# A two-layer encoder trunk: the pooling's scale and bias arrive as single rows and are spread by TensorE, the first filler matmuls run on a memset tile, and the constant table moves to SP's queue

## The reference, cut to what matters

```
h = rms_norm(x, norm_mix[0])
pooled[g] = mean of h over the last 2/4/8/16 tokens - h      # four groups of 256 channels
mixed[g]  = pooled[g] @ pool_w[g] + pool_b[g]                 # 256 x 256 per group
x = x + mixed * pool_scale                                    # pool_b and pool_scale: 1024 numbers each
h = rms_norm(x, norm_ffn[0]); x = x + (silu(h @ w1) * (h @ w3)) @ w2
```

## Time and profile before

| | |
|---|---|
| median of three runs | 1173.79 us |
| lowest, highest | 1169.85, 1173.88 us |
| the profiled execution: its own time | 1170.22 us |
| its span | 1168.4 us |
| TensorE matmul busy | 93% of the span |
| VectorE, ScalarE, GpSimd busy | 28%, 20%, 3% |
| HBM read | 414.09 MB, 356 GB/s over the span |

### The profile page before, as it was taken

How to read it: one execution, slowest core, us unless ns; L and a number is a source line. 1 busy time by engine, 2 the same in 40 slices (tenths; PEclk the granted TensorE clock), 3 DMA queues, 4 the chain that set the end, 5 groups by cost and what they waited for, 6 DMA issues and landing times.

```text
span 1168.4 us, 25208 instructions
## 1 busy us (share of the span) xinstructions
PE 1090.7 (93%) x11721; PEld 616.5 (53%) x11721; DVE 328.9 (28%) x455; ACT 236.6 (20%) x370; POOL 39.4 (3%) x35
## 2 busy tenths in 40 slices
PE   7999999999999999999999869999997889999776
PEld 6888888889763354364455215333632444364233
DVE  5655555458660040040032004002200310050023
ACT  5586555656620000000000000000000000000002
POOL 3000000011000000000000000000000000000000
PEclk9999999999999999999999999999999899999989
DMA  9986556534379999999999999999999999999994
GB/s 349 386 300 208 184 193 203 180 126 158 119 306 411 423 404 425 426 421 427 423 429 421 425 429 419 428 424 429 420 425 426 422 426 424 427 424 423 428 423 163
DMA packets 58562, 417.88 MB, mean 358 GB/s; under 512 B 5730, under 2 KB 11924, under 8 KB 34004
## 3 DMA queue, kind: packets, MB, share of 16 engines
q1 hardware_dynamic: 56656, 411.21, 86.3%
q0 software_dynamic: 1440, 4.46, 1.0%
q10 hardware_dynamic: 356, 0.54, 0.1%
HBM read 414.09 MB, written 2.10 MB: 356 GB/s over the span
## 4 chain that ended last, share of the span: by engine, by line
PE 64%; DMA 33%; SPq 2%; DVE 1%; issue 0%; ACT 0%; DVEq 0%
DMA weights<-in_moe_w 32%; PE psum L865 23%; PE psum L908 13%; PE psum L771 8%; PE psum L773 8%; PE psum L772 8%; SPq L682 1%; DMA raw<-in_pool_w 1%; PE psum L991 1%; PE psum L779 0%; PE psum L1112 0%; PE psum L883 0%; PE psum L1089 0%; SPq L673 0%; PE psum L1058 0%
## 5 line engine op out<-in xcount | busy, mean ns | idle before, releaser
L865 PE MATMUL psum<-weights,xg 128*32 128x512 f32 (+1 forms) x5072 | 494.8, 549 | 52.7 <-DMA weights<-in_moe_w 52.6
L865 PEld LDWEIGHTS psum<-weights,xg 128*32 128x32 f32 x5072 | 176.6, 111 | 368.4 <-issue 325.8
L908 PE MATMUL psum<-weights,hid_t 128*32 128x256 f32 x4480 | 247.7, 379 | 6.1 <-DMA weights<-in_moe_w 6.0
L908 PEld LDWEIGHTS psum<-weights,hid_t 128*32 128x32 f32 x4480 | 148.8, 110 | 99.8 <-DMA weights<-in_moe_w 9.1
L1718 DVE TENSOR_TENSOR sil<-sil,psum 128x1536 f32<-128x1536 f32 (+3 forms) x16 | 21.1, 1321 | 500.2 <-PE psum L865 499.5
L1572 DVE TENSOR_TENSOR low<-raw,high 128x2048 fp32r<-128x2048 f32 x50 | 114.3, 2286 | 95.5 <-ACT high L1276 95.3
L1276 ACT ACTIVATE high<-raw 128x2048 fp32r<-128x2048 f32 x51 | 97.8, 1917 | 54.4 <-PE psum L773 51.0
L1342 ACT ACTIVATE y_hi<-psum 128x768 fp32r<-128x768 f32 (+1 forms) x7 | 5.0, 719 | 488.6 <-PE psum L908 488.6
L771 PE MATMUL psum<-high,a_hi 128*128 128x512 f32 x224 | 87.3, 390 | 0.9 <-DVE a_lo L1609 0.9
L773 PE MATMUL psum<-low,a_hi 128*128 128x512 f32 x224 | 87.2, 389 | 0.0
L772 PE MATMUL psum<-high,a_lo 128*128 128x512 f32 x224 | 87.2, 389 | 0.0
(11 more groups left out here) (246 smaller groups left out, 676.1 us busy)
## 6 DMA issues: line engine op xcount, KB each, us to landing
weights<-in_moe_w SPq DMA_DIRECT2D x128, 1792.0 KB, 36.0
weights<-in_moe_w SPq DMA_DIRECT2D x47, 2048.0 KB, 38.7
raw<-in_ffn_w SPq DMA_DIRECT2D x42, 1024.0 KB, 8.7
weights<-in_moe_w SPq DMA_DIRECT2D x16, 1024.0 KB, 38.0
raw<-in_w_q SPq DMA_DIRECT2D x4, 1024.0 KB, 5.1
raw<-in_w_o SPq DMA_DIRECT2D x4, 1024.0 KB, 4.9
weights<-in_moe_w SPq DMA_DIRECT2D x4, 512.0 KB, 35.6
x_res<-in_x SPq DMA_DIRECT2D x2, 512.0 KB, 5.4
```

The source lines that it names most:

```text
L865: mm = pe.matmul(UP[c][g * BLK:(g + 1) * BLK, r, :], xg[:, k_, r * BLK:(r + 1) * BLK], w[:, g], start=k_ == 0, stop=k_ == DT - 1)
L908: mm = pe.matmul(Y[g * BLK:(g + 1) * BLK, to, :], hid_t[c][:, r, at_:at_ + BLK], w[:, b, g * GW:(g + 1) * GW], start=i == 0 and b == 0 and ...
```

## The change

- The table leaves ACT's queue and is issued on SP's, behind the band matrices.
- `pool_scale` and `pool_b` are no longer copied to 128 partitions. Each is loaded as one row of 4 KB into partition 0, by ACT's queue, as its first two DMAs.
- VectorE fills a new tile `filler` (128 x 256) with ones, ahead of its two small memsets, and multiplies the two rows on partition 0 before the norm.
- TensorE starts when the filler is written: two matmuls of 256 columns on it; a wait for the rows; two matmuls of 512 columns that spread the scale over 128 partitions (a row of ones against the row) into banks 6 and 7; a wait for VectorE's product; two that spread the product into banks 4 and 5; three more fillers. The eight matmuls on the identity are gone.
- ScalarE copies the spread product from banks 4 and 5 to `pool_bs`; its two copies of the scale to PSUM are gone, and so is GpSimd's product.
- The turned vectors go to bank 3 rather than 5, so TensorE waits for their copy before its seventh pair of pooling matmuls; it waits for ScalarE's copy of the product before the mixing matmuls.

```diff
+        filler = at("filler", [P, SEQ], F32, o_w + 8 * K)
...
             sp.dma_start(raw[slot(U_BAND)][:, 0:len(WINDOWS) * BAND], bands).then_inc(landed[slot(U_BAND)], 16)
+            sp.dma_start(consts[:, 0:C_COS], table[:, 0:C_COS]).then_inc(consts_in, 16)
             vector_loads(sp, 0, 2)
-            sp.dma_start(pool_rows[:, 1, :], bc(pool_scale[0])).then_inc(scale_in, 16)
             load(U_POOLW, pool_w.rearrange("o g (k p) f -> p (o g k) f", p=P), 8)
-            sp.dma_start(pool_rows[:, 0, :], bc(pool_b.rearrange("o g d -> (o g d)"))).then_inc(pool_in, 16)
...
-            pool.wait_ge(scale_in, 16)
-            pool.wait_ge(pool_in, 16)
-            pool.tensor_tensor(pool_bs[:], pool_rows[:, 0, :], pool_rows[:, 1, :], ALU.mult).then_inc(pool_ready, 1)
-            pool.wait_ge(pool_ready, 1)
+            pool.wait_ge(bias_copied, 1)
             pool.wait_ge(xn_ready, NT)
             pool.tensor_tensor(x_res[:, 1, :], x_res[:, 1, :], pool_bs[:], ALU.add).then_inc(pool_ready, 1)
...
+            def fill(n):
+                for _ in range(n):
+                    pe.matmul(banks[0][:, 0:SEQ], filler[:, 0:P], filler[:], start=True, stop=True)
+            pe.wait_ge(dve_step, 1)
+            fill(2)
+            pe.wait_ge(rows_in, 32)
+            for half in range(2):
+                pe.matmul(banks[OUT[1][half]][:], filler[0:1, 0:P], pool_rows[0:1, 1, half * CW:(half + 1) * CW],
+                          start=True, stop=True).then_inc(rows_spread, 1)
+            pe.wait_ge(dve_step, 3)
+            for half in range(2):
+                pe.matmul(banks[OUT[0][half]][:], filler[0:1, 0:P], pool_bs[0:1, half * CW:(half + 1) * CW],
+                          start=True, stop=True).then_inc(rows_spread, 1)
+            fill(3)
             pe.wait_ge(consts_in, 16)
-            keep_warm(0, 8)
             pe.wait_ge(xn_ready, NT)
...
+                if d == 5:
+                    pe.wait_ge(gains_ready, 1)
                 if d == 0:
                     pe.wait_ge(vec_in, 16 * 7)
-                    pe.transpose(banks[5][:, 0:NV], vec_rows[:, :], ident[0:NV, 0:NV]).then_inc(vec_turned, 1)
+                    pe.transpose(banks[3][:, 0:NV], vec_rows[:, :], ident[0:NV, 0:NV]).then_inc(vec_turned, 1)
             pe.wait_ge(pooled, DT // 2)
             pe.wait_ge(landed[slot(U_POOLW)], 16)
-            pe.wait_ge(gains_ready, 1)
+            pe.wait_ge(bias_copied, 1)
...
-            act.dma_start(consts[:, 0:C_COS], table[:, 0:C_COS]).then_inc(consts_in, 16)
-            act.wait_ge(dve_step, 1)
+            act.dma_start(pool_rows[0:1, 1, :], pool_scale[0].rearrange("(o n) -> o n", o=1)).then_inc(rows_in, 16)
+            act.dma_start(pool_rows[0:1, 0, :], pool_b.rearrange("o g d -> o (g d)")).then_inc(rows_in, 16)
+            act.wait_ge(dve_step, 2)
             warm(ACT.Sqrt)
             vector_loads(act, 2, 7)
             norm(0, lambda t: (x_in[t], 16))
-            act.wait_ge(scale_in, 16)
-            for half in range(2):
-                act.activation(banks[OUT[1][half]][:], pool_rows[:, 1, half * CW:(half + 1) * CW],
-                               ACT.Copy).then_inc(scale_spread, 1)
+            act.wait_ge(rows_spread, 4)
+            act.activation(pool_bs[:], psum[:, OUT[0][0] * CW:(OUT[0][1] + 1) * CW], ACT.Copy).then_inc(bias_copied, 1)
...
+            step(dve.memset(filler[:], 1.0))
             dve.memset(eps, EPS)
             step(dve.memset(warm_in, 1.0))
+            dve.wait_ge(rows_in, 32)
+            step(dve.tensor_tensor(pool_bs[0:1, :], pool_rows[0:1, 0, :], pool_rows[0:1, 1, :], ALU.mult))
...
-                dve.wait_ge(scale_spread, h + 1)
+                dve.wait_ge(rows_spread, h + 1)
...
-            dve.wait_ge(pool_ready, 1)
+            dve.wait_ge(bias_copied, 1)
             step(dve.tensor_tensor(x_res[:, 0, :], x_res[:, 0, :], pool_bs[:], ALU.add))
```

More of the change, by code:

```diff
@@ L408, in trunk_program @@
         x_in = [sem(f"x_in{t}") for t in range(NT)]
-        consts_in, vec_in, pool_in = sem("consts_in"), sem("vec_in"), sem("pool_in")
+        consts_in, vec_in, rows_in = sem("consts_in"), sem("vec_in"), sem("rows_in")
         misc_in, bo_in, rope_in = sem("misc_in"), sem("bo_in"), sem("rope_in")
@@ L421, in trunk_program @@
         pool_ready, pooled, mixed = sem("pool_ready"), sem("pooled"), sem("mixed")
-        scale_in, scale_spread, w_scaled = sem("scale_in"), sem("scale_spread"), sem("w_scaled")
+        rows_spread, w_scaled, bias_copied = sem("rows_spread"), sem("w_scaled"), sem("bias_copied")
         pooled_even, pooled_odd = sem("pooled_even"), sem("pooled_odd")
@@ L1743, in _ @@
             dve.wait_ge(vec_turned, 1)
-            dve.tensor_copy(gains[:], banks[5][:, 0:NV]).then_inc(gains_ready, 1)
+            dve.tensor_copy(gains[:], banks[3][:, 0:NV]).then_inc(gains_ready, 1)
             dve.wait_ge(gains_ready, 1)
@@ L1762, in _ @@
                 if t:
-                    dve.wait_ge(pool_ready, 2)
+                    dve.wait_ge(pool_ready, 1)
                 for half in range(2):
```

## The result

The changed kernel is slower: 1175.37 us median (1174.39 to 1176.48, 11 runs) against 1172.36 for the kernel before (1169.85 to 1173.88, 11 runs). The ratio is 1.003, with a 95% interval of 1.0021 to 1.0038, which is 2.5 to 4.5 us. The forecast was a gain of 0.85. The time lies inside the range that was given, and inside 0.5%, but on the other side: what came true is the first rival, by its clock that stays low.

What follows compares the result with a forecast made beforehand. The start chain to the first dense matmul was taken to bound, passing through one for one; weights gain 1.30, but TensorE's pooling limits mixing's gain to 0.85, so median 1173.79 - 0.85 = 1172.9 us, range 1168.5 to 1176.2.

Steps and rivals of the forecast that it cites:

- the first rival: Late rows (+2.3 us) or a clock that stays low (+2.7) make TensorE's start the bound; both +5.2; chance 0.22.
- The bound, and one for one to the end: TensorE's progress releases the late weight stream, so what the first 25 us win or lose reaches the end in full.
- the rise of the clock: TensorE's start: fast level after some 3.5 us of matmuls, at 4.65 or 7.1; TensorE free at 8.95 or 10.15, middle 9.55.
- I price them by columns: Spreading matmuls over one partition: 512 columns cost 0.86 us per record at the low clock, 0.43 at the high.
- signs of being wrong: Spreading records of 0.86 throughout, first pooling matmul after 10.4, early gain gone at 497, or over 6 us from behind 26.
- (a): Pooling weights landed and scaled before mixing: landing at 12.14, scaled by 13.45, mixing possible at 13.6; gain 1.30 us.
- x and the table: Start loads: table no longer shares engines with x; tile 0 lands at 4.97, norm done at 9.16, 0.65 us earlier.
- Rows: Two 4 KB loads on ACT's queue, expected landed at 3.6 us, between bounds of 3.56 and 6.16.
- VectorE and SP's queue: VectorE's row product takes 1.23 us, ending at 4.9; SP issues weights about where they were, dense units 2.3 earlier.
- GpSimd's first low part: Second chain before the first dense matmul: ends near 21.5 instead of 25.25, 3 us to spare; no further gain.
- (c): ScalarE's copy of the spread product before mixing: about 1.1 us, done by 10, costs 0.
- (b): TensorE through with pooling before mixing: pooling from 9.55 to 13.95, mixing at 14.05, a gain of 0.85 us.

## Why the prediction was wrong, point by point

- **The bound, and one for one to the end: right.** The table above carries it for gains and losses.
- **The step that failed is TensorE's: the rise of the clock, counted 3.5 us from the first filler or from the rows, with the spreading taken as work that brings it up.** The other half, "I price them by columns", holds at either level: 0.85 low, 0.43 high. The Trainium skill (TensorE: Matmul & The Clock Gate, "Why this matters for your kernels") says that a matmul with a contraction of 32 takes the time of one with 128. The spreading at the high level, with six fillers ahead, agrees down to one partition: 587 ns against 592 at full height. The forecast put the rise between 4.65 and 7.1; it came at 15.7, after the late fillers had begun. From the rows to a free TensorE the forecast counted 5.95 us (3.6 to 9.55), and 10.05 passed (4.22 to 14.27); pooling, part of it low, took the rest. Two of the prediction's own signs of being wrong showed: spreading records of 0.86 throughout, and a first pooling matmul after 10.4.
- **The height is not all of it.** At full height and with the rows at their old time mixing still began 2.27 later than the 14.05 of the forecast. There spreading began at 4.54 and not at 3.6, and the clock rose in a record that began 4.4 us after that, not 3.5. The two early fillers, 1.27 us of idle time ahead of the rows, did not bring the rise forward in this trace, so of the two counts the one from the first filler did not hold with that gap. With four fillers and no gap the rise fell in a record that began at 5.7 instead of 9.0.
- **The first rival had the place and the condition.** Its price for a clock "low to the end" was mixing 2.7 us later, with late rows on top 5.2; measured were 4.34. It counted 4.5 from a free TensorE to mixing, which took 4.97 (14.27 to 19.24) as the first part of pooling was low, and 0.86 and 0.43 for records that took up to 0.95 and 0.48. It was given 0.22, and the height of the contraction was not among the reasons for it. Neither late rows nor the gap kept the clock low to the end of spreading: the rows were in at 4.17, and full height behind a like gap had the clock up for the record of 9.81 (593 ns).
- **(a) Weights: right in direction, the term mis-sized.** 1.30 us was bytes at a rate; landing moved by 2.4, 0.24 of it from an earlier issue, and the copy issued again costs 2.9. It bought nothing, because (b) ended last.
- **x and the table: mis-sized.** The norm was done 1.27 earlier, not 0.65, and x tile 0 was awaited until 4.34. By the Trainium skill (DMA: Bandwidth & Descriptors, "Issuing engines are not separate DMA queues") a second issuing engine saves only the time of issuing; the prediction read that as a move worth nothing, which leaves out the order of the loads. Here, with the table behind the bands and the rows in its old place, x came 1.28 earlier, and 0.9 to 1.3 over all traces (5.48 and 5.62 before, 4.33 to 4.57 with the table moved). No run moved the table alone. The table landed at 7.95, under the norm, as said.
- **Rows: near.** 4.17 against 3.6, 2.86 us after the second issue. The prediction's side estimate with 2.0 us by the Trainium skill (DMA: Bandwidth & Descriptors, "Anatomy of one DMA") was farther off; that section gives the figure for loads that GpSimd issues, and these were issued by ACT's queue.
- **VectorE and SP's queue: as said, GpSimd in part.** The product took 1.22 on one partition; the seven vectors' copy held up nothing. GpSimd's first low part ended at 26.47 (21.93 + 4.54) and not near 21.5, as ScalarE's high part came behind the late pooling; it kept 3.1 us to the first dense matmul because that was late too.
- **(c) and ScalarE: wrong in degree.** Its copy waited 3.90 us for spreading and came at 11.44, but pooling came later still, so it cost nothing.
- **The late fillers: a term that was priced at the high level, 1.37.** They took 2.86 on the path, and leaving them out started mixing 1.64 sooner.
- **What a measurement can tell: more than was said.** The prediction took 5.9 us as the least that shows; the interval of the ratio is 2.0 us wide, and a loss of 2.5 to 4.5 us stands clear of no change. That the time lies in the range is luck: the range allows for a loss of 2.3 us, 3.0 came, and it held because it starts from the highest run.

## What to carry to other kernels

Matmuls that contract over one partition cost by their columns and, in these runs, neither raised TensorE's clock nor held it; ahead of real work they cost twice, once at the low level and once more in what follows. If a row must be spread by TensorE early, let it contract over zeroed partitions at full height, start fillers as soon as a memset tile stands, let them run on until the work without a gap, and put none between the last wait and the work. When work leaves the DMA queues for the engine that is second to the bound, add up that engine's new path at both clock levels before counting the transfer as gained.

## What the runs showed of the hardware that was not expected

- The clock fell under one-partition matmuls that ran without a gap: 587 ns per record from 5.6 us, 964 and then 1052 from about 8 us (six fillers ahead).
- The time from the first of an unbroken run of full-height matmuls to the first shortened record differed from trace to trace: 2.7 us (before once more), 3.1 (six fillers ahead), 3.4 (before, and late fillers left out), 4.3 (changed), 4.4 (both runs with two early fillers and full height), 4.5 (four fillers ahead), 5.7 (copied scale issued again).
- A copy of one 4 KB row to 128 partitions, 512 KB, put off the landing of the next load by 2.9 us, 2.5 without the later issue, where 512 KB at the 402 GB/s of the earlier trace rows is 1.30.
- The granted clock read 1.00 through stretches in which every record had the length of the low level.
